# A two-block transformer on one core: row factors, gate curves and split activations moved within their engines' orders

## The reference

```
x = x + 0.5 * swiglu(rmsnorm(x, ffn1_norm), ffn1_w_gu, ffn1_w_down)
z = rmsnorm(x, mix_norm) @ w_in
y_a = spatial_gating(gelu(z_u), gelu(z_v), ...)
y_b = mla(z_cq, z_ckv, z_kr, positions, ...)     # 8 causal heads; q and k are rms-normed per row, and turned by angles
y_c = memory_attention(z_qm, mem, ...)           # 4 heads
gates = sigmoid(z_gate + b_gate)                 # three branches of 1024 features
merged = gates[0] * (y_a @ w_branch_a) + gates[1] * (y_b @ w_branch_b) + gates[2] * (y_c @ w_branch_c)
x = x + merged @ w_out
x = x + 0.5 * swiglu(rmsnorm(x, ffn2_norm), ffn2_w_gu, ffn2_w_down)
```

## Time and profile before

| | |
|---|---|
| median of 3 runs | 1633.46 us (1633.15 to 1638.04) |
| the profiled execution | 1632.28 us, span 1630.4 us |
| PE busy | 1559.5 us (96% of the span) |
| DVE, ACT, POOL busy | 1067.9, 802.7, 371.5 us |
| mean granted clock of TensorE | 0.984 |
| the chain that ended last, by engine | PE 77%, DVE 8%, issue 7%, ACT 6%, DMA 2% |

### The profile page before, as it was taken

One profiled execution on the slowest core, in us unless ns is written; L12 is line 12 of the kernel. 1 busy time (PEld: TensorE's weight loads), 2 busy tenths in 40 slices (PEclk: granted clock), 3 DMA queues, 4 the chain that ended last, 5 costly groups with the idle time before them and its releaser, 6 DMA issues.

```text
span 1630.4 us, 33714 instructions
## 1 busy us (share of the span) xinstructions
PE 1559.5 (96%) x13961; PEld 1480.4 (91%) x13961; DVE 1067.9 (65%) x1531; ACT 802.7 (49%) x1211; POOL 371.5 (23%) x376
## 2 busy tenths in 40 slices
PE   6999999899999999999999999999899898899998
PEld 6898988689899998988999999999896798899998
DVE  6785465484788746656888566666566665666654
ACT  6764333554555546545555545344543247354332
POOL 0014442023266520002366311120000000212110
PEclk9998899999999999999999999999999999999999
DMA  7463120353455455622454555545633532545553
GB/s 260 160 190 102 42 68 3 134 206 129 146 178 180 142 168 181 209 91 104 158 181 157 177 193 199 188 158 181 222 104 130 207 125 96 194 156 200 178 168 123
DMA packets 42797, 252.21 MB, mean 155 GB/s; under 512 B 5648, under 2 KB 7808, under 8 KB 20928
## 3 DMA queue, kind: packets, MB, share of 16 engines
q1 hardware_dynamic: 38704, 233.20, 41.9%
q0 software_dynamic: 3984, 17.46, 3.9%
HBM read 249.47 MB, written 1.17 MB: 154 GB/s over the span
## 4 chain that ended last, share of the span: by engine, by line
PE 77%; DVE 8%; issue 7%; ACT 6%; DMA 2%; POOL 0%; ACTq 0%; SPq 0%; DVEq 0%; POOLq 0%
PE bank L426 21%; PE bank L428 21%; PE bank L427 21%; PE bank L1250 3%; DVE w_lo L299 3%; ACT w_hi L296 2%; DMA sq<-rows_scratch_q 1%; PE bank L628 1%; ACT work L2498 1%; DVE rs L581 1%; DVE mix L587 1%; PE bank L1420 0%; DVE w_spare L1323 0%; PE bank L1412 0%; PE bank L1427 0%
## 5 line engine op out<-in xcount | busy, mean ns | idle before, releaser
L426 PE MATMUL bank<-work_r,w_hi 128*128 128x256 f32 (+2 forms) x3248 | 924.9, 285 | 21.0 <-DVE w_lo L299 10.9
L427 PE MATMUL bank<-work_r,w_hi 128*128 128x256 f32 (+2 forms) x3248 | 917.5, 282 | 0.0
L428 PE MATMUL bank<-work_r,w_lo 128*128 128x256 f32 (+2 forms) x3248 | 917.0, 282 | 0.0
L299 DVE TENSOR_TENSOR w_lo<-ring,w_hi 128x2048 fp32r<-128x2048 f32 (+2 forms) x233 | 498.1, 2139 | 317.1 <-ACT w_hi L296 317.0
L426 PEld LDWEIGHTS bank<-work_r,w_hi 128*128 128x128 f32 x3248 | 616.1, 190 | 34.7 <-DVE w_lo L299 14.9
L296 ACT ACTIVATE w_hi<-ring 128x2048 fp32r<-128x2048 f32 (+2 forms) x233 | 408.5, 1754 | 459.6 <-PE bank L428 459.4
L427 PEld LDWEIGHTS bank<-work_r,w_hi 128*128 128x128 f32 x3248 | 616.1, 190 | 0.2
L428 PEld LDWEIGHTS bank<-work_r,w_lo 128*128 128x128 f32 x3248 | 616.2, 190 | 0.0
L1637 POOL TENSOR_TENSOR work<-work 128x272 f32<-128x272 f32 (+1 forms) x44 | 92.8, 2110 | 136.7 <-ACT work L1599 136.7
L537 POOL TENSOR_TENSOR sq<-sq 128x256 f32<-128x256 f32 (+2 forms) x36 | 57.5, 1598 | 207.8 <-ACT sq L515 207.0
L1625 DVE SCALAR_TENSOR_TENSOR work<-work,params_sb 128x272 f32<-128x272 f32 (+1 forms) x176 | 99.5, 606 | 5.1 <-DVE work L1625 0.3
(11 more groups left out here) (452 smaller groups left out, 1688.6 us busy)
## 6 DMA issues: line engine op xcount, KB each, us to landing
ring<-in_stream SPq DMA_DIRECT2D x164, 1024.0 KB, 4.9
ring<-in_stream SPq DMA_DIRECT2D x64, 704.0 KB, 4.0
ring<-in_stream SPq DMA_DIRECT2D x10, 768.0 KB, 4.3
work<-rows_scratch POOLq DMA_DIRECT2D x12, 512.0 KB, 5.8
ring<-in_stream SPq DMA_DIRECT2D x7, 512.0 KB, 3.7
work<-rows_scratch POOLq DMA_DIRECT2D x4, 544.0 KB, 6.3
work<-rows_scratch_o POOLq DMA_DIRECT2D x1, 2176.0 KB, 9.3
work<-rows_scratch_m POOLq DMA_DIRECT2D x1, 1088.0 KB, 7.4
```

What stands on the lines that cost most here:

```text
L299: eng.tensor_tensor(w_lo[:, slot, 0:size], raw_w, w_hi[:, slot, 0:size].bitcast(F32), ALU.subtract).then_inc(lo_done, 1)
L426: pe.matmul(out, w_hi[:, slot, at:at + P], hi, start=first, stop=False)
L427: pe.matmul(out, w_hi[:, slot, at:at + P], lo, start=False, stop=False)
L428: mm = pe.matmul(out, w_lo[:, slot, at:at + P], hi, start=False, stop=last)
```

## The change

- `prepare` of up0 and up1 stands ahead of the eight `input_act` on ACT.
- The angles are computed in five pieces at slabs 4, 6, 8, 10 and 12 of down2. The Sin table is loaded in the body of product 5 and the sine taken in the body of product 7 (a product has two slabs), each ahead of that body's wait; the Sqrt table is loaded behind `prepare` of in_uv.
- On DVE the 16 reciprocals stand ahead of `mem_rows_dve`. The factors come back in four transfers: rows 0 and 1 of q and of k, then the other six of each; pair 0 waits for the first two alone.
- The second branch's split moves from slab 11 to slab 10 on ACT, and on DVE from behind the phase to slab 11. ACT applies the sigmoid to block 0 at slab 11, to block 1 behind the last head, and to block j + 2 in branches' slab j.
- `M_HI` and `M_LO` of block c are made in branches, two slabs behind.

```diff
-        def residual_input_act(act, name, gain_of, between=None):
-            each_product(act, name, 1, lambda un: (un.was_read(act), input_act(act, un.j, gain_of)), turns=0, split="hi", end="hold", between=between)
+        def residual_input_act(act, name, gain_of, beside=None):
+            def body(un):
+                if beside is not None:
+                    beside(un.j)
+                un.was_read(act)
+                input_act(act, un.j, gain_of)
+            each_product(act, name, 1, body, turns=0, split="hi", end="hold")
+        def rope_beside_act(act, j):
+            if j == 5:
+                act.preload_act_table(ACT.Sin)
+            if j == 7:
+                rope_act(act)
...
-            i, quarter = ((2, 0.0), (3, 0.25))[part - 1]
-            inc(dve.tensor_scalar(t(1), t(0), 1.0 / (2 * np.pi), quarter, ALU.mult, ALU.add))
...
+            i, quarter = ((2, 0.0), (3, 0.25))[(part - 1) // 2]
+            if part % 2:
+                inc(dve.tensor_scalar(t(1), t(0), 1.0 / (2 * np.pi), quarter, ALU.mult, ALU.add))
+                own()
+                inc(dve.tensor_scalar(t(4), t(1), ROUND, None, ALU.add))
+                own()
+                inc(dve.tensor_scalar(t(1), t(4), -ROUND, None, ALU.add))
+                return
...
         def rope_act(act):
             act.wait_ge(*S.at("rope_dve", "args"))
-            act.preload_act_table(ACT.Sin)
             S.inc(act.activation(trig[0:QK, 2:4, :], trig[0:QK, 2:4, :], ACT.Sin), "rope_act")
-            act.preload_act_table(ACT.Sqrt)
...
-            dve.wait_ge(S.sem("mla_rows_in"), 32)
+            dve.wait_ge(S.sem("mla_pair_in" if pairs == (0,) else "mla_rows_in"), 32)
...
-            pool.dma_start(sq_q, on_all(scr_q, 0, (SEQ, 8), (1, SEQ))).then_inc(S.sem("mla_rows_in"), 16)
-            pool.dma_start(sq_k, on_all(scr_q, 8 * SEQ, (SEQ, 8), (1, SEQ))).then_inc(S.sem("mla_rows_in"), 16)
+            for lo, n, arrived in ((0, 2, "mla_pair_in"), (2, 6, "mla_rows_in")):
+                for dst, row0 in ((sq_q, 0), (sq_k, 8)):
+                    pool.dma_start(dst[:, lo:lo + n, :], on_all(scr_q, (row0 + lo) * SEQ, (SEQ, n), (1, SEQ))).then_inc(S.sem(arrived), 16)
...
+                if j == 10:
+                    act.wait_ge(*S.at("att_act", "o7"))
+                    split_branch_act(act, 1)
                 if j == 11:
                     act.preload_act_table(ACT.Sigmoid)
-                    act.wait_ge(*S.at("att_act", "o7"))
-                    split_branch_act(act, 1)
-                    phase_read(act, "in_gates", 22)
-                    for c in range(3):
-                        gate_curve(act, c)
+                    phase_read(act, "in_gates", 20)
+                    gate_curve(act, 0)
...
-            for c in range(3, DB):
-                gate_curve(act, c)
+            gate_curve(act, 1)
+        def branches_act(act):
+            each_product(act, "branches", 3, lambda un: gate_curve(act, un.j + 2) if un.j + 2 < DB else None, turns=0, split="hi",
+                         late=lambda un: merged_act(act, un.j), lag=2, split_last=True)
...
+                if j == 11:
+                    split_branch_dve(dve, 1)
...
-            split_branch_dve(dve, 1)
...
-            each_product(dve, "branches", 3, body, turns=0, split="lo", split_last=True)
+            each_product(dve, "branches", 3, body, turns=0, split="lo", split_last=True, late=lambda un: merged_dve(dve, un.j), lag=2)
+        def merged_act(act, c):
+            if c == 0:
+                S.begin("x_hi")
+            act.wait_ge(*S.at("merge_pool", c))
+            S.inc(act.activation(M_HI[:, c, :], merged[:, c, :], ACT.Copy), "x_hi", c)
+        def merged_dve(dve, c):
+            if c == 0:
+                S.begin("x_lo")
+            dve.wait_ge(*S.at("x_hi", c, 9))
+            S.inc(dve.tensor_tensor(M_LO[:, c, :], merged[:, c, :], M_HI[:, c, :].bitcast(F32), ALU.subtract), "x_lo", c)
...
+                prepare(act, "hi", f"up{layer}")
                 for k in range(DB):
                     act.wait_ge(*S.at("norm_add", k, 2 * layer))
                     input_act(act, k, gain("norm_w", (4 * layer + 2) * DB), MIXED[layer])
-                prepare(act, "hi", f"up{layer}")
...
-            residual_input_act(act, "down2", gain("mix_norm"), lambda slab: rope_act(act) if slab == 12 else None)
+            residual_input_act(act, "down2", gain("mix_norm"), lambda j: rope_beside_act(act, j))
             prepare(act, "hi", "in_uv")
+            act.preload_act_table(ACT.Sqrt)
...
-            each_product(act, "branches", 3, nothing, split="hi")
-            split_act(act, 9, merged, M_HI, 8, SEQ, ready=lambda k: act.wait_ge(*S.at("merge_pool", k)))
+            branches_act(act)
...
-                     lambda slab: rope_dve(dve, {4: 0, 6: 1, 8: 2}[slab]) if slab in (4, 6, 8) else None)
+                     lambda slab: rope_dve(dve, slab // 2 - 2) if slab in (4, 6, 8, 10, 12) else None)
...
+            rown_dve(dve, 3, SEQ, 16)
             mem_rows_dve(dve)
-            rown_dve(dve, 3, SEQ, 16)
...
-            split_dve(dve, 9, merged, M_HI, M_LO, 8, SEQ)
```

## The result

The changed kernel takes 1611.06 us (median of 4 runs, 1605.92 to 1618.27) beside 1635.6 us for the kernel before (median of 4, the 3 runs above and one more): ratio 0.9855, 95% interval 0.982 to 0.989. Timed again with six runs, the ratio is 0.9853 (0.982 to 0.988). The forecast was 1609.7 us, in a range of 1604 to 1618: faster, and by the amount predicted. That the median lies 1.4 us from the forecast is in part luck: the four runs are two pairs 8 to 12 us apart (1605.92 and 1606.91, 1615.2 and 1618.27), and the median falls between them.

A forecast was written before the change was run, and what follows sets the result against it. PE was taken as the bound, winning time only at waits between phases and half-clock stretches behind them. Terms of 2.7, 5.6, 6.1, 6.3 and 3.1 summed to 23.8 us: 1608.5, or 1609.7 for a median, range 1604 to 1618.

The forecast's parts named there:

- up0 and up1: Second slab's w_hi made before the inputs removes PE's 1.33 us wait in each: 2.7 us, bounds 0 and 2.7.
- down2: Angles in five pieces and moved table loads remove waits of 0.77 and 3.19 us plus 1.7 of clock: 5.6 us.
- row factors: Attention: factors sent 3.9 us sooner, first pair split off, DVE's 6.11 us wait goes: 6.1 us, bounds 3.9 and 6.7.
- end of in_gates to slab 2: Spread gate curves give 3.2 us at head 11's turn, 1.7 of clock, 1.37 at slab 2: 6.3 us.
- inside branches: Added sigmoids, casts and subtractions fit ACT's and DVE's free time in each slab: cost 0, bounds 0 and 4 us.
- mix_out: Its start: ready M_HI and M_LO shorten PE's 5.30 us wait, one clock fall stays: 3.1 us, bounds 2.0 and 4.9.
- the cover: up0 and up1: ACT makes w_hi (1.90 us) within its 3.22 us idle before the first norm_add, delaying no input_act.
- Its limit: Attention: PE could gain more, but its first turn needs DVE's first softmax, so the gain was taken as 6.1 us.
- The step by which the pair should be early: Attention: the first pair, a quarter of the bytes, lands in near 4.5 us, long before DVE needs it.
- second rival: Attention: the pair lands no sooner than the whole, gain 3.9 us or less, 1611.9 us; chance 0.08.
- first rival: At the waits removed: the clock falls stay, gain only 17.9 us, 1615.6 us; chance 0.13.
- third rival: Branches: Sigmoid and Copy switch tables twice a slab, ACT's turn is 5.8 us against 4.1, 1623.3 us; chance 0.03.

The follow-up runs named there:

- loads back: Changed kernel with down2's Sin and both table loads at slab 12, up0/up1 prepare behind the inputs: 5.01 us longer at slab 14, up0 1.60, up1 1.72.
- No-swap: Changed kernel with the reciprocals behind the products of mem_rows again, the split transfers kept: attention stage 4.24 us longer.
- three lots: Changed kernel with the angles' five pieces in three lots at slabs 4, 6 and 8 of down2: 0.86 us longer at slab 8.
- again: The changed kernel itself, unedited, timed once more beside the kernel before: six runs in all, 1604.55 to 1615.22 us, median 1612.5.
- whole rows: Changed kernel with the row factors sent as two whole transfers, still behind the earlier reciprocals: attention stage 0.00 us apart.
- curves back: Changed kernel with three gate curves at slab 11, five behind the last head, none in branches: 4.53 us longer at in_gates' end, 1.50 to slab 2.
- all steps: Changed kernel plus earlier last merged halves, last head's turn earlier, heads 1 to 3 behind first softmax: median 1605.58 us, ratio to before 0.9816.

## Why the prediction was right, step by step

| term | forecast | measured |
|---|---|---|
| up0 and up1 | 2.7 | 1.60 + 1.71 = 3.3 |
| down2 | 5.6 | 0.87 + 4.74 = 5.6 |
| row factors | 6.1 | 6.6 |
| end of in_gates to slab 2 | 6.3 | 4.60 + 1.79 = 6.4 |
| inside branches | 0 | 0.0 |
| mix_out | 3.1 | 3.1 |
| sum | 23.8 | 25.0 |

- up0 and up1: the cover was right, and the 3.3 us lie over its upper bound of 2.7. Each stage gave 0.3 to 0.4 us more than the 1.33 us read at up0; up1's own wait is longer, 1.50 us with the loads back.
- down2: right in its parts, and the loads were the main one (5.0 of 5.6). The prediction's opening line that PE waits at junctions and not inside phases doesn't fit here: the waits at slab 8 and 14 stand inside down2. The Trainium skill (ScalarE: Activation LUTs, "What ACT_TABLE_LOAD costs") adds about 1.38 us of drain to a load. The trace does not agree with that: in the changed kernel the instruction ahead of the load ends as the load starts, the load ends at 1140.17, and ACT then idles 0.73 us, put down to DVE.
- Row factors: the sum was near, 6.1 for 6.6. PE's waits in the stage went from 5.43 us (3.92, 1.18 and two short ones) to 1.59, and the fall of the clock gave back the other 2.8; the prediction left out the second wait, of 1.18 us. Its limit was real: the first turn now waits for DVE's softmax, 1.02 us. The step by which the pair should be early was not right. "a quarter on the quiet queue I put near the second" (4.5 us): it took 6.7. What carried the gain was the swap, which the text held possible ("the split may be needless"). The second rival's mechanism, parts that land no sooner than the whole, was nearly true (6.7 against 7.5 us; the ring loads that it puts on the same queue are issued by SP, the rows by POOL), but its price, 3.9 us or less of gain, was wrong: sent sooner, whole rows are in time.
- End of in_gates: the wait came out at 1.51 us for 1.6 forecast, and the clock stayed at 1.00 behind it, as taken from the earlier trace rows. The first rival (the clock doesn't come back) fails here and in attention and down2. No-swap shows that it wasn't empty: there two waits of 1.18 and 1.28 us did bring a fall.
- mix_out: the waits left are 0.41 and 2.46 us, for the two of 3.3 us forecast; the first is for `w_lo`, not for M_LO. One fall was forecast and is in the profile, but of the seven traces with this wait of 2.46 us four have the fall (the changed kernel, no swap, loads back, three lots) and three don't (again, whole rows, curves back). The 1.7 us for it were right as a price, not as a certainty: without the fall, in the second trace, the stage gains 4.5 us, so that 3.1 for 3.1 is luck.
- ACT's turn in branches: no load between Copy and Sigmoid, no wait of PE; the third rival fell. One turn of the changed kernel, with ACT waiting for PE ahead of it:

```profile
1368.62 1.49 ACT L296 ACTIVATE w_hi<-ring 128x1536 fp32r<-128x1536 f32 x1 [1.39 <-PE bank L428]
1370.01 1.29 ACT L2511 ACTIVATE work<-work,params_sb 128x256 f32<-128x256 f32 x3
1371.21 0.40 ACT L2586 ACTIVATE work_r<-work 128x256 fp32r<-128x256 f32 x1
```

## What to carry to other kernels

Read a gain at the junction where PE stands still, and add the half-speed stretch behind it: about half of down2's wait again, and two thirds of what no-swap lost, was clock. Send a transfer sooner before splitting it, and measure the parts apart. Compare stages between the same matmuls, since untouched stages moved whole runs by more than any single edit gained.

## What the runs showed of the hardware that was not expected

- Two pitches at the same granted clock. In up3 and down3 of the changed kernel 170 us hold 1445 matmuls, of its second trace 1501, both with granted clock 1.00 and DMA share 0.50: 117.6 against 113.3 ns a matmul. Successive starts are 117 to 119 ns apart in the one and, but for a handful, 113 to 114 in the other, and a run switches between the levels: in the changed kernel the slower one holds from 1426 us to the end; elsewhere it lasted from 6 to over 120 us. What sets it stays open. The other engines keep their times: the 128x2048 `w_lo` takes 2.54 us in the one stretch and 2.53 in the other, the `w_hi` 1.92 in both.
- The scan (140 to 180 us), which nothing here touches, differs by 8.0 us between traces (6.28 us under the changed kernel's in curves back, 1.76 over it with all steps): the longer stage has more of its time at 0.50. With the pitch this is enough for the 12 us between the fastest and the slowest of four runs, though only one of these has a trace.
- A late 1024 KB transfer took 10.9 us, the same sent 3.7 us sooner (against DVE's need of it) 7.5, and a 256 KB one in its place 6.7: here the bytes mattered less than when it was sent. Why the late one took longer stays open.
